# Token lists of the experts: made one by one on TensorE and VectorE, or written once into a table in DRAM

## What is computed

```python
logits = (xt @ w_router + b_router).astype(jnp.float32)
top_val, top_idx = lax.top_k(logits, TOP_K)          # TOP_K = 4 of N_EXPERTS = 32
gate_w = jax.nn.softmax(top_val, axis=-1)
...                                                  # rows of a block belong to one expert e
h = clamped_swiglu(xe @ w_gate[e] + b_gate[e], xe @ w_up[e] + b_up[e])
yb = h @ w_down[e] + b_down[e]
out = jnp.zeros_like(xt).at[token_of].add(yb[dest] * gate_w)
x2 = layer_norm(DEEPNORM_ALPHA * x1 + out, ln2_g, ln2_b)
```

## Time and profile before

| | us |
|---|---|
| median of 3 runs | 1460.9 (1460.77 to 1462.64) |
| profiled execution, its time | 1461.05 |
| profiled execution, its span | 1459.1 |
| TensorE busy | 1393.9 (96%) |
| VectorE busy | 468.0 (32%) |
| ScalarE busy | 325.3 (22%) |
| GpSimd busy | 115.3 (8%) |

### The profile page before, as it was taken

The page is one execution under the profiler, slowest core; times in us unless marked ns, Lnnn a source line. Parts: engine busy times, 40 slices in busy tenths (PEclk is TensorE's granted clock), DMA queues, the critical chain, the costliest instruction groups (busy, mean ns, idle before and its releaser), DMA issues.

```text
span 1459.1 us, 37797 instructions
## 1 busy us (share of the span) xinstructions
PE 1393.9 (96%) x16616; PEld 946.7 (65%) x16616; DVE 468.0 (32%) x891; ACT 325.3 (22%) x668; POOL 115.3 (8%) x119
## 2 busy tenths in 40 slices
PE   6999999997999999999999999999999999999991
PEld 5777776555566666666666666666666666666660
DVE  3245556364422223222222222222222222222224
ACT  3544466121021111111111211111111111111114
POOL 1022000001001000000000010001000000100000
PEclk9999999996999999999999999999999999999996
DMA  7211032566999999999999999999999999999944
GB/s 246 89 49 44 15 120 92 210 235 261 362 402 395 396 387 396 398 396 388 398 400 398 397 399 397 389 396 400 397 386 399 398 397 400 397 399 386 396 165 143
DMA packets 78468, 463.93 MB, mean 318 GB/s; under 512 B 12400, under 2 KB 13632, under 8 KB 29008
## 3 DMA queue, kind: packets, MB, share of 16 engines
q1 hardware_dynamic: 67616, 429.54, 73.9%
q0 software_dynamic: 10192, 31.31, 8.4%
q10 hardware_dynamic: 512, 0.79, 0.1%
HBM read 444.70 MB, written 22.22 MB: 320 GB/s over the span
## 4 chain that ended last, share of the span: by engine, by line
PE 90%; DVE 4%; ACT 2%; DMA 2%; issue 1%; DVEq 0%; POOL 0%; SPq 0%; ACTq 0%; POOLq 0%
PE unit L1248 42%; PE unit L1251 27%; PE unit L1157 4%; PE unit L1231 2%; PE unit L756 2%; PE unit L758 2%; PE unit L757 2%; PE unit L1236 2%; PE unit L751 1%; PE unit L1175 1%; DMA xbuf<-x_prompt_dram 1%; PE unit L908 1%; PE unit L884 1%; PE unit L791 1%; DVE attT L2175 1%
## 5 line engine op out<-in xcount | busy, mean ns | idle before, releaser
L1248 PE MATMUL unit<-ring_b,xeT 128*32 128x512 f32 (+1 forms) x3168 | 353.5, 488 | 1.1 <-ACT xeT L1411 1.1
L1251 PE MATMUL unit<-ring_b,xeT 128*32 128x256 f32 x1584 | 354.0, 381 | 0.0
L1251 PE MATMUL unit<-ring_a,xeT 128*32 128x256 f32 x1488 | 330.7, 379 | 0.0
L1248 PE MATMUL unit<-ring_a,xeT 128*32 128x256 f32 (+1 forms) x2976 | 330.2, 486 | 0.0
L1251 PEld LDWEIGHTS unit<-ring_b,xeT 128*32 128x32 f32 x1584 | 171.4, 110 | 56.3 <-issue 0.7
L1251 PEld LDWEIGHTS unit<-ring_a,xeT 128*32 128x32 f32 x1488 | 161.8, 110 | 52.5
L1251 PE MATMUL unit<-ring_a,heT 128*32 128x256 f32 x768 | 169.7, 379 | 0.0
L1248 PE MATMUL unit<-ring_a,heT 128*32 128x512 f32 (+1 forms) x1536 | 169.4, 486 | 0.0
L1248 PEld LDWEIGHTS unit<-ring_b,xeT 128*32 128x32 f32 x3168 | 126.5, 110 | 60.4 <-issue 4.3
L1251 PE MATMUL unit<-ring_b,heT 128*32 128x256 f32 x720 | 160.3, 379 | 0.0
L1248 PE MATMUL unit<-ring_b,heT 128*32 128x256 f32 (+1 forms) x1440 | 160.1, 486 | 0.0
(11 more groups left out here) (322 smaller groups left out, 1601.5 us busy)
## 6 DMA issues: line engine op xcount, KB each, us to landing
ring_b<-w_gate_dram SPq DMA_DIRECT2D x68, 1024.0 KB
ring_a<-w_down_dram SPq DMA_DIRECT2D x68, 1024.0 KB
ring_b<-w_up_dram SPq DMA_DIRECT2D x64, 1024.0 KB
ring_a<-w_up_dram SPq DMA_DIRECT2D x64, 1024.0 KB
ring_a<-w_gate_dram SPq DMA_DIRECT2D x60, 1024.0 KB
ring_b<-w_down_dram SPq DMA_DIRECT2D x60, 1024.0 KB
raw_a<-w_in_dram SPq DMA_DIRECT2D x16, 512.0 KB, 3.6
xbuf<-x_prompt_dram SPq DMA_DIRECT2D x4, 512.0 KB, 5.4
```

The lines of the kernel that those rows point to most:

```text
L1248: return mm(out[j * NS:(j + 1) * NS, a:b], stat(j), w[:, a:b], start=first, stop=last)
L1251: return mm(out[CAP:P, j * 256:(j + 1) * 256], stat(j), w[:, FOLD:D], start=start, stop=stop)
```

## The change

`LISTED` = 6. The first six experts get their lists as before. For experts 6 to 31 the lists come from a table `lists` in DRAM, 96 slots x 32 experts of int32, with room behind it for entries that are over 96.

- At the beginning GpSimd fills the table with the numbers of free slots, from a new input `no_rows`.
- Behind the routing VectorE computes for every token and choice the place in the table: slot x 32 + expert, or a place in the spill area where the slot is 96 or more (`place`, 128 x 5 x 4), and the token numbers `tokid`. `idxf` becomes `idxfs`, one per tile, so that it is still there.
- GpSimd writes the table with 20 indirect stores (`enter`), one for each tile and choice, one int32 per partition: ten in `pool_step(0)` and ten in `pool_step(1)`, each time behind the wait for `y_stored`.
- In `pool_step(2)` it waits until all have landed and loads columns 6 to 31 of `idx` with one DMA; the gather of expert 6 waits for it (`lists_in`). `idx` has 32 columns now, so that no `read_rows` waits for `y_free`.
- TensorE, VectorE: no pick and no wait for one from expert 6 on. GpSimd's steps are written out, not looped.
- ACT waits for `go4` to be filled where it waited for `s_read`, whose semaphore `lists_in` takes.

```diff
@@ constants and tiles
+LISTED = 6
-        idxf = sb("idxf", [P, TOPK])
+        idxfs = sb("idxfs", [P, NT, TOPK])
-        idx = sb("idx", [P, TURN], I32)
+        idx = sb("idx", [P, NE], I32)
+        lists_dram = nc.dram_tensor("lists", (CAP * NE + NT * P * TOPK, 1), I32, kind="Internal").ap()
@@ gpsimd
+            pool.dma_start(lists_dram[0:CAP * NE].rearrange("(s e) a -> s (e a)", e=NE), d["no_rows"][:, :]).then_inc(out_done, 16)
...
+            def enter(some):
+
+                pool.wait_ge(mask_ready, NT + 1)
+                for i, k in some:
+                    r = rows(i)
+                    pool.indirect_dma_start(lists_dram, bass.IndirectOffsetOnAxis(ap=place[:r, i, k:k + 1], axis=0),
+                                            tokid[:r, i:i + 1], None).then_inc(out_done, 16)
+
...
-                if not isinstance(e, int) or e < NE - 2:
-                    pool.wait_ge(idx_ready, e + 3)
+                if e < NE - 2:
+                    if e + 2 < LISTED:
+                        pool.wait_ge(idx_ready, e + 3)
+                    elif e + 2 == LISTED:
+                        pool.wait_ge(lists_in, 16)
...
-            for e in range(TURN):
-                pool_step(e, e, e == 0)
-            with pool.Fori(1, NE // TURN - 1) as it:
-                for par in range(TURN):
-                    pool_step(it * TURN + par, par)
+            entries = [(i, k) for i in range(NT) for k in range(TOPK)]
+            for e in range(LISTED - 2):
+                pool_step(e, e == 0)
+                if e < 2:
+                    enter(entries[e * 10:(e + 1) * 10])
+                if e == 2:
+                    pool.wait_ge(out_done, 16 * (OUTS + NT * TOPK))
+                    pool.dma_start(idx[:CAP, LISTED:NE], lists_dram[0:CAP * NE].rearrange("(s e) a -> s (e a)", e=NE)
+                                   [:, LISTED:NE]).then_inc(lists_in, 16)
@@ tensor, pe_step
-                if not no_more:
+                if e + 2 < LISTED:
                     pe.wait_ge(picked, e + 3)
                     pe.wait_ge(gate_read, e + 2)
                     rows_of(tok_done, CAP)
@@ scalar
-            act.wait_ge(s_read, 1)
+            act.wait_ge(*filled("go4"))
@@ vector
+            st(tt(onehot[:], onehot[:], posm[:].unsqueeze(2).to_broadcast([P, NT, TOPK, NE]), ALU.mult))
+            tokv = k_("tokv").rearrange("p (t c) -> p t c", c=3)
+            st(tt(tokid[:], tokv[:, :, 0], tokv[:, :, 1], ALU.add))
...
+            st(red(placef[:], onehot[:], ALU.add))
...
+            st(ts(over[:], placef[:], float(CAP), None, ALU.is_ge))
+            st(stt(placef[:], placef[:], float(NE), idxfs[:], ALU.mult, ALU.add))
...
+            st(tt(onehot[:, :, :, 0], spill, placef[:], ALU.subtract))
...
+            st(tt(over[:], over[:], onehot[:, :, :, 0], ALU.mult))
...
+            st(tt(place[:], placef[:], over[:], ALU.add))
...
+            v.sem_inc(mask_ready, 1)
...
-                if not no_more:
-                    v.wait_ge(y_free, e + 1)
-                    read_rows(e + 2, (par + 2) % TURN)
-                    if not (isinstance(e, int) and e >= NE - 3):
-                        col = posm[:, :, e + 3:e + 4] if isinstance(e, int) else posm[:, :, bass.ds(e + 3, 1)]
-                        pick_rows(col).then_inc(picked, 1)
+                if isinstance(e, int) and e + 2 < LISTED:
+                    read_rows(e + 2, e + 2)
+                    if e + 3 < LISTED:
+                        pick_rows(posm[:, :, e + 3:e + 4]).then_inc(picked, 1)
```

More of the change, by code:

```diff
@@ L47 @@
 XCOLS = D + NE
-KEEP = dict(ident=P, iota=P, tokv=NT * 3, slot=4, jcol=MAXEXTRA)
+LISTED = 6
+KEEP = dict(ident=P, iota=P, tokv=NT * 3, slot=4, jcol=MAXEXTRA, spill=NT * TOPK)
 EARLY = dict(cum=P, rest=P, cum_s=NS, rest_s=NS, before=P, ones=P, upto32=2 * NE, cos=NT * ROT, sin=NT * ROT,
@@ L310, in build @@
         xpos = sb("xpos", [P, NT])
+        tokid = sb("tokid", [P, NT], I32)
+        place = sb("place", [P, NT, TOPK], I32)
+        placef = sb("placef", [P, NT, TOPK])
+        over = sb("over", [P, NT, TOPK])
         assert here[0] <= qkv_at + 2 * D * 4
@@ L434, in build @@
         sample_dve, sample_act, selo = (sem(n) for n in ("sample_dve", "sample_act", "selo"))
-        state_ready, sstate_ready, s_read, s_decayed, rms_ready, mix_ready = (sem(n) for n in (
-            "state_ready", "sstate_ready", "s_read", "s_decayed", "rms_ready", "mix_ready"))
+        state_ready, sstate_ready, lists_in, s_decayed, rms_ready, mix_ready = (sem(n) for n in (
+            "state_ready", "sstate_ready", "lists_in", "s_decayed", "rms_ready", "mix_ready"))
         var_ready, std_ready, x1_ready, x1T_ready, ntop_ready, g_exp, mask_ready, xb_ready = (
@@ L694, in add_rows, with pool_step @@
                                                compute_op=ALU.add)
[L696 to L699 removed]
+            def enter(some):
[4 more added lines that the diff above has]
+                                            tokid[:r, i:i + 1], None).then_inc(out_done, 16)
+            def pool_step(e, first=False):
+                if e < NE - 2:
[3 more added lines that the diff above has]
+                        pool.wait_ge(lists_in, 16)
                     pool.wait_ge(xT_done, e + 2)
@@ L703, in pool_step @@
                     pool.sem_inc(turn_over, 1)
-                    gather(par + 2)
+                    gather(e + 2)
                 if first:
@@ L710, in pool_step @@
                 pool.sem_inc(turn_over, 1)
-                add_rows(ysb[:CAP], idx[:CAP, par:par + 1]).then_inc(y_stored, 16)
+                add_rows(ysb[:CAP], idx[:CAP, e:e + 1]).then_inc(y_stored, 16)
                 pool.wait_ge(y_stored, e * 16 + 16)
                 pool.sem_inc(y_free, 1)
-            for e in range(TURN):
-                pool_step(e, e, e == 0)
-            with pool.Fori(1, NE // TURN - 1) as it:
-                for par in range(TURN):
-                    pool_step(it * TURN + par, par)
+            entries = [(i, k) for i in range(NT) for k in range(TOPK)]
[7 more added lines that the diff above has]
+                                   [:, LISTED:NE]).then_inc(lists_in, 16)
             n_extra = pool.value_load(itab[0:1, MAXEXTRA:MAXEXTRA + 1], min_val=0, max_val=MAXEXTRA)
-            for e in range(NE - TURN, NE):
-                pool_step(e, e % TURN)
+            for e in range(LISTED - 2, NE):
+                pool_step(e)
             with pool.If(n_extra > 0):
@@ L2618 @@
         [per_expert[:, :, 0:FOLD]] * 3 + [np.tile(per_expert[:, :, FOLD:D], (1, 1, 3))], 1))
+    arrays["no_rows"] = np.ascontiguousarray(np.broadcast_to(T + np.arange(CAP, dtype=np.int32)[:, None], (CAP, NE)))
     arrays["sinkrow"] = np.ascontiguousarray(np.tile(np.repeat(arrays["swa_sinks"][0], DEC), 4)[:, None])
@@ L2622 @@
     for name, a in arrays.items():
-        d[name] = nc.dram_tensor(f"{name}_dram", a.shape, F32, kind="ExternalInput").ap()
+        d[name] = nc.dram_tensor(f"{name}_dram", a.shape, I32 if name == "no_rows" else F32, kind="ExternalInput").ap()
     d["cache_k"], d["cache_v"] = d["cache_swa_k"], d["cache_swa_v"]
```

18 lines of the change are left out of this document (13 added, 5 removed).

## The result

The changed kernel takes 1471.8 us in the median of four executions (1468.19 to 1474.36); the kernel before, beside it, 1460.84 (1458.61 to 1462.64). The ratio is 1.0072, with a 95% interval from 1.0053 to 1.0091: slower, by 0.5 to 0.9%. The forecast was 1457.6 us and faster; 1471.8 lies within its range, on the other side of the kernel before. The profiled execution is the fastest of the four: 1468.19 us, span 1466.4.

The account below looks back on a forecast made before the run. TensorE was taken to bound the kernel, with DMA close behind. Picks removed -4.9, VectorE's added work +0.2 and late gathers +1.4 gave -3.3 us, from 1460.9 to 1457.6 us; the range was 1455 to 1476 us.

Parts of the forecast that it names:

- Part 1: TensorE, experts 6 to 31: 26 groups of five pick matmuls go, 0.19 us each, a gain of 4.9 us.
- rival 3: Weight stream: faster TensorE finds its weight pieces late, so the 4.9 us turn into waits, 1461 us; chance 0.10.
- Parts 2 and 3: VectorE: removed picks and readings worth 0; eight added instructions before the first product, 2.7 us against 2.95 slack, cost 0.2 us.
- Part 4: GpSimd's queue: two batches of ten stores delay gathers 3 and 4 by 0.8 and 1.4 us; loss 1.4 us.
- as bytes nothing: DMA traffic: stores of some 9 KB and table filling of 12 KB, against 16.20 MB moved in 40 us, cost nothing.
- Rival 1: DMA engines, 415 to 490 us: store rows queue for turns among weight packets, gathers 3 and 4 late, 1483 us; chance 0.18.
- Rival 2: GpSimd: a store's issue grows with its rows to 1.94 us, gather 3 8.7 us late, 1464.9 us; chance 0.16.

Follow-up runs that it names:

- no_stores: Changed kernel without its 20 stores, table filled at the beginning with fixed lists of 68 tokens per expert; 1460.3 us.
- thin: Changed kernel with stores one at a time, behind each gather and addition of experts 0 to 9, picks for the first twelve experts; 1460.7 us.
- mild execution: The first profiled execution of the changed kernel, nothing altered, the fastest of its four; 1468.19 us.
- only_half: stores_only with only the first ten of the 20 stores, those that follow expert 0; 1470.8 us.
- only_apart: stores_only with every destination index multiplied by 128, so rows lie 512 bytes apart in a table of 2.9 MB; 1469.2 us.
- stores_behind: Changed kernel with the 20 stores behind the gathers of experts 3 and 4 on GpSimd's queue instead of ahead of them; 1476.3 us.
- after_again: The changed kernel unaltered, run once more for one more profiled execution; 1479.8 us.
- only_inner: only_direct with the same 20 DMAs of 128 four-byte rows going into columns of an SBUF tile instead of DRAM; 1460.7 us.
- only_wide: only_direct with each of the 20 plain DMAs writing 128 rows of 512 bytes to DRAM instead of 4 bytes; 1462.8 us.
- stores_only: Kernel before, all picks kept, plus the 20 stores, the added VectorE work and the list load into a tile nobody reads; 1481.1 us.
- only_direct: stores_only with the 20 indirect stores replaced by plain DMAs of the same rows to fixed consecutive rows of the table's tail; 1479.7 us.
- after: The changed kernel itself, here its first profiled execution; median 1471.8 us, this execution 1468.19 us.
- the skip: Additions to acc_rows leave out each expert's free list slots by bounds_check; 1460.6 us on the kernel before, 1461.3 us on no_stores.

## Why the prediction was wrong

- **Part 1** was right: 33.29 us from step 6 on, 0.19 us per pick. Of the 4.9 us, 2.4 are lost at the end; rival 3 had this mechanism, and I gave it 0.10. It holds for half of the gain, in no_stores and thin as well.
- **Parts 2 and 3** were right. The eight instructions on VectorE run from 347.74 to 350.45, 2.7 us as worked out, and the first product starts at 352.10 (352.20 before); step 1 is 0.2 us longer, which is no more than it differs between the runs; no gap stands at steps 5 and 6, where the loaded table is first used.
- **Part 4 is the step that failed.** It forecast a loss of 1.4 us, the larger of two late gathers. In the mild execution gather 3 is late by (429.43 - 415.79) + 3.5 - 10.7 = 6.4 us, the wait that TensorE has. Two terms of that sum were mis-sized: the store at 1.15 us, when 1.27 us pass from one to the next (0.97 busy, which was below my guess, and 0.30 between them, which I had left out), and the landing, which I carried over as 8.5 us and which became 12.0. Gather 4 held nobody up, so that the two do not add, as I wrote; but a third loss was not in the sum at all: behind the wait TensorE runs at the lower clock, 2.9 us in step 4. That is 9.4 us in place of 1.4. The same pair, a wait and then a lower clock, stands in only_half (6.1 and 1.3 us) and only_apart (3.8 and 2.4).
- **What Part 4 did not contain at all** is the sentence "as bytes nothing". I priced the stores' transfer by bytes. stores_behind and after_again show a cost with no waiting gather in it, 18 to 21 us in steps 3 and 4, and only_inner and only_wide show what it hangs on: small writes to DRAM. A rule that speaks of this stands in the Trainium skill, and I had not weighed it: "DMA: Bandwidth & Descriptors", section "Specifications", has transfers under 512 bytes become read-modify-write, and its section "Why small descriptors are slow (HBM only)" spares SBUF. The runs agree with both (18 us for 4 bytes, 1.4 us for 512 bytes, which is within the noise, none into SBUF); but rows of 4 bytes that lie 512 bytes apart are under 512 bytes too, and with them the traffic kept its 419 GB/s, so the size is not the whole rule here. That other queues and TensorE pay along, the page doesn't say.
- **Rival 1** had the right place and the wrong cause. It had the rows wait for turns among weight packets. The packets are as few as the Trainium skill has it ("DMA: Bandwidth & Descriptors", section "Queues, rings and completion order"): queue q0 has 704 packets more, which is 20 stores of 16 packets (of 32 bytes, and of 8 for the last tile) and 16 completions, plus 64 for fill and load. That rule spoke against the rival, which I gave 0.18; but a packet count says nothing of what happens to the packets beside them. Its 1483 us is near after_again's 1479.8, but not by its mechanism: only_inner makes as many turns and loses nothing.
- **Rival 2** fell: 0.97 us for 128 rows and 0.87 for 32.
- **The range** holds the measured 1471.8 us by luck. It was drawn up to 1476 for the milder part of rival 1, one gather that comes 15 us late; the mechanism that put the time there was in none of the rivals. (Two sums are slightly off: the chances add up to 0.28 within 0.2% and 0.30 slower, and a store of 1.0 us for all rows would already make gather 4 late by 0.5 us.)

That bursts of four-byte writes to DRAM, close together, are the cause is shown by experiments. That TensorE's slowness in the bad executions comes of the same is shown too (only_inner, only_wide and no_stores don't have it); by which path it reaches TensorE is open. Its weights were there, and no wait is recorded. Late instruction fetches would be a path. In stores_only the fetches lie at 415.1 and 436.5 us, 21 us apart, where before they are 8 to 11 apart. But TensorE is back at its pace from 431 on, ahead of the second, which looks as if the fetches followed TensorE there. The path isn't excluded: in only_direct a long fetch (3.2 us) stands beside the gap, and in after_again one lands at 433.6, just as the pace comes back. Whether the slowness also happens when nothing is recorded was not tried.

## What to carry to other kernels

Price a small DMA to DRAM by the kind of its write, not by its bytes or its issue: in a burst beside a full stream, a store of 128 rows of 4 bytes costs about 0.9 us, as a direct or an indirect DMA. Write whole rows of 512 bytes, or into SBUF, or one such store at a time with 10 to 23 us between them, as thin does. Price a wait of TensorE with the lower clock that can follow it: here 2.9 us behind 6.4. When a DMA share is full, read the GB/s beside it, and count the lead of a prefetch as something that a disturbance spends: in only_direct it was missed 650 to 900 us later.

## What the runs showed of the hardware

- 20 DMAs of 128 rows of 4 bytes cost 18 us when written to DRAM (rows in a few KB), 8 us with the rows 512 bytes apart (in the trace 3.8 of them a wait for the gather behind them, 2.4 the clock), and nothing measurable into SBUF or as rows of 512 bytes.
- While they run, 8192-byte packets of another queue take up to 5.5 us (at most 0.86 in the same 10 us of before), and TensorE can fall to 31 matmuls in 10 us from 136, with no wait on record.
- While TensorE stood for 6.4 us (after, 435.1 to 441.5), its granted clock fell to 0.50 at 438.0; it rose again at 448.2, 6.7 us after TensorE went on, and that step took 2.9 us longer.
- Where the skip took the packets of 29% of the added rows away, those of the weight stream took 1.4% longer each, and the DMA share stayed full.
